# Rotary swap of two attention layers through small transfers, a turn of the identity ahead of long rows of products, and weight halves split earlier on VectorE

## What is computed

```python
def _rope(x, cos, sin):                 # q and k, heads of 64
    x1, x2 = jnp.split(xf, 2, axis=-1)  # halves of 32
    out = jnp.concatenate([x1 * c - x2 * s, x2 * c + x1 * s], axis=-1)
...
for l in range(DEPTH):                  # 2 layers
    h = _swiglu(x, ffn_w1[l, 0], ffn_w3[l, 0], ffn_w2[l, 0])
    x = _layernorm(ALPHA * x + 0.5 * h, ...)
    h = _mixer(x, l, ...)               # z = x @ w_in; q, k = _rope(q), _rope(k); ...
    x = _layernorm(ALPHA * x + h, ...)
    h = _swiglu(x, ffn_w1[l, 1], ffn_w3[l, 1], ffn_w2[l, 1])
    x = _layernorm(ALPHA * x + 0.5 * h, ...)
...                                     # second block: six chunks of silu(c) @ w_mod
```

## Time and profile before

| | us |
|---|---|
| median of three runs | 1831.58 |
| lowest, highest | 1826.11, 1833.10 |
| the profiled execution | 1825.48 |
| its span, on which the trace's times lie | 1823.6 |
| PE busy (98% of the span) | 1789.7 |
| DVE busy (62%) | 1136.4 |
| ACT busy (48%) | 867.9 |
| POOL busy (14%) | 247.0 |

### The profile page before, as it was taken

One profiled execution on the slowest core, in us unless ns is written; L12 is line 12 of the kernel. 1 busy time (PEld: TensorE's weight loads), 2 busy tenths in 40 slices (PEclk: granted clock), 3 DMA queues, 4 the chain that ended last, 5 costly groups with the idle time before them and its releaser, 6 DMA issues.

```text
span 1823.6 us, 31041 instructions
## 1 busy us (share of the span) xinstructions
PE 1789.7 (98%) x12819; PEld 1617.9 (89%) x12819; DVE 1136.4 (62%) x1735; ACT 867.9 (48%) x1412; POOL 247.0 (14%) x264
## 2 busy tenths in 40 slices
PE   9999999999999999999999999999999999999999
PEld 8998699999899879996899997999776877879999
DVE  5754587676766466655675876566655655565553
ACT  5454344664444435443535753545345355445543
POOL 2000232121200020001231212000111443100000
PEclk9999999999999999999999999999999999999999
DMA  8665654545666666754755455775443433346663
GB/s 285 195 219 192 233 186 159 165 139 191 206 208 209 204 208 231 231 185 161 250 169 185 135 168 193 234 242 182 165 152 93 110 98 93 117 159 190 203 194 111
DMA packets 252396, 330.56 MB, mean 181 GB/s; under 512 B 13162, under 2 KB 213072, under 8 KB 252256
## 3 DMA queue, kind: packets, MB, share of 16 engines
q1 hardware_dynamic: 248240, 315.31, 53.2%
q0 software_dynamic: 4016, 13.27, 2.1%
HBM read 327.51 MB, written 1.05 MB: 180 GB/s over the span
## 4 chain that ended last, share of the span: by engine, by line
PE 64%; issue 24%; DVE 6%; POOL 2%; ACT 2%; DMA 1%; POOLq 0%; DVEq 0%; ACTq 0%
PE bank L714 14%; PE bank L717 14%; PE bank L715 14%; PE bank L737 5%; PE bank L739 5%; PE bank L740 5%; DVE X L1930 1%; DVE wlo L1852 1%; ACT whi L1402 1%; PE bank L1250 1%; PE bank L1272 1%; POOL rs L2447 1%; DMA G<-in_lam_dram 1%; PE bank L898 1%; PE bank L936 1%
## 5 line engine op out<-in xcount | busy, mean ns | idle before, releaser
L1852 DVE TENSOR_TENSOR wlo<-raw,whi 128x1024 fp32r<-128x1024 f32 x537 | 663.8, 1241 | 374.6 <-ACT whi L1402 370.5
L1402 ACT ACTIVATE whi<-raw 128x1024 fp32r<-128x1024 f32 x549 | 574.4, 1052 | 393.6 <-PE bank L740 171.7
L714 PE MATMUL bank<-XTh,whi 128*128 128x256 f32 x1984 | 560.7, 283 | 0.0
L717 PE MATMUL bank<-XTh,wlo 128*128 128x256 f32 x1984 | 551.8, 278 | 2.9 <-DVE wlo L1852 2.9
L715 PE MATMUL bank<-XTl,whi 128*128 128x256 f32 x1984 | 551.6, 278 | 0.0
L717 PEld LDWEIGHTS bank<-XTh,wlo 128*128 128x128 f32 x1984 | 372.9, 188 | 3.3 <-DVE wlo L1852 3.3
L715 PEld LDWEIGHTS bank<-XTl,whi 128*128 128x128 f32 x1984 | 374.8, 189 | 1.0
L714 PEld LDWEIGHTS bank<-XTh,whi 128*128 128x128 f32 x1984 | 372.9, 188 | 2.9
L714 PE MATMUL bank<-HCh,whi 128*128 128x256 f32 (+1 forms) x880 | 252.5, 287 | 0.9 <-DVE tmp L2343 0.9
L717 PE MATMUL bank<-HCh,wlo 128*128 128x256 f32 (+1 forms) x880 | 248.1, 282 | 0.0
L715 PE MATMUL bank<-HCl,whi 128*128 128x256 f32 (+1 forms) x880 | 248.1, 282 | 0.0
(11 more groups left out here) (342 smaller groups left out, 2419.6 us busy)
## 6 DMA issues: line engine op xcount, KB each, us to landing
raw<-in_ffn_w_dram SPq DMA_DIRECT2D x131, 1024.0 KB, 5.1
raw<-in_w_in_dram SPq DMA_DIRECT2D x76, 1024.0 KB, 5.0
raw<-in_w_mod_dram SPq DMA_DIRECT2D x24, 1024.0 KB, 5.0
raw<-in_w_branch_dram SPq DMA_DIRECT2D x16, 1024.0 KB, 5.0
raw<-in_w_out_dram SPq DMA_DIRECT2D x12, 1024.0 KB, 4.9
raw<-in_w_ffn_gate_dram SPq DMA_DIRECT2D x11, 1024.0 KB, 5.1
raw<-in_w_ffn_up_dram SPq DMA_DIRECT2D x11, 1024.0 KB, 5.1
raw<-in_w_ffn_down_dram SPq DMA_DIRECT2D x8, 1024.0 KB, 5.1
```

Of the source, the lines that this page charges most:

```text
L714: e.matmul(o, hi[:, k, w0:w0 + nc_], xh, start=first and k == 0, stop=False)
L717: m = e.matmul(o, lo[:, k, w0:w0 + nc_], xh, start=False, stop=last and k == nk - 1)
L1402: e.activation(hi_part(n), raw_part(n), ACTF.Copy).then_inc(WHI.did(n), 1)
L1852: e.tensor_tensor(lo_part(n), raw_part(n), hi_part(n).bitcast(F32), ALU.subtract).then_inc(WLO.did(n), 1)
```

## The change

Three things.

1. **Rotary.** `perm` and its product are gone. The swap of partitions p and p^32 is made by four DMAs of 32 partitions x 256 numbers (32 KB each) from the copy `s` to a buffer `u` of `mtmp`: two are issued by SP (partitions 0 to 63) and two by POOL (64 to 127). The ring has six buffers in place of four. SP issues them between two loads of weights, POOL ahead of its additions. DVE multiplies the copy by cos (`times_cos(n-1)`) and one group later the swapped copy by sin (`times_sin(n-2)`); POOL adds `rotate(n-2)`. ACT's copy of group n now waits for the four DMAs of group n-3.
2. **A turn of the identity.** `settle(b)` transposes the 128 x 128 identity into an unused part of a bank: at the end of each `modulation`, and in each mixer between V and the first q/k group.
3. **Splits ahead of long work on DVE.** `sum_up` does half of a chunk at a time, so a split stands between the halves. `w.more(1)` is called ahead of the second layernorm tile of V on ACT and DVE, and ahead of `g2` on ACT and DVE.

The core of the diff:

```diff
             if self.summed and self.summed[0] < min(self.parts[self.n][0], self.loaded):
-                c = self.summed.pop(0)
-                self.done.add(c)
+                c = self.summed[0]
                 if self.sum_up:
-                    self.sum_up(c)
-                self.load()
+                    self.sum_up(c, self.step)
+                self.step = 1 - self.step
+                if self.step == 0:
+                    self.done.add(self.summed.pop(0))
+                    self.load()
...
+            def turned(l, n):                       # SP
+                ring_free(q, tm[l], ("u", n))
+                q.wait_ge(AMX, ("qk", l, n))
+                for p in (0, 32):
+                    e.dma_start(mtmp[tm[l].slot["u", n]][p:p + 32, :], mtmp[tm[l].slot["s", n]][p ^ 32:(p ^ 32) + 32, :]).then_inc(
+                        ROT[n % 4].did(("turned", l, n), by=16), 16)
...
             for c in range(1, before_bias):
                 load(c)
+                for l in range(2):
+                    if first_qk[l] <= c - 4 < first_qk[l] + 8:
+                        for j in range(2):
+                            turned(l, 2 * (c - 4 - first_qk[l]) + j)
...
+            def settle(b):                          # PE
+                return e.transpose(bank[b][:, 256:384], ident, ident)
...
-                mm.then_inc(MOD.did(("columns", g)), 1)
+                settle(b).then_inc(MOD.did(("columns", g)), 1)
...
+                empty(3)
+                settle(3)
                 for n in range(16):
                     b = n % 4
                     empty(b)
                     gemm_a(bank[b][:, 0:T], xt, ("qk", l, n))
                     emptied[b] = ((AMX, ("qk", l, n)),)
-                    if n:
-                        rotate(n - 1)
...
                 for n in range(16):                 # DVE
                     w.pass_by(1)
                     if n:
-                        rotate(n - 1)
+                        times_cos(n - 1)
+                    if n > 1:
+                        times_sin(n - 2)
+                times_cos(15)
...
+                def turned(n):                      # POOL
+                    ring_free(q, tm[l], ("u", n))
+                    q.wait_ge(AMX, ("qk", l, n))
+                    for p in (64, 96):
+                        e.dma_start(mtmp[tm[l].slot["u", n]][p:p + 32, :], mtmp[tm[l].slot["s", n]][p ^ 32:(p ^ 32) + 32, :]).then_inc(
+                            ROTP[n % 4].did(("turned", l, n), by=16), 16)
                 for n in range(16):
                     w.pass_by(1)
-                    if n:
-                        rotate(n - 1)
+                    turned(n)
+                    if n > 1:
+                        rotate(n - 2)
```

More of the change, by code:

```diff
@@ L379, in program @@
     with ctx:
-        chunks, parts, whole, on_dve, before_bias = plan(I)
+        chunks, parts, whole, on_dve, before_bias, first_qk = plan(I)
         of_chunk = {}
@@ L393, in program @@
         BIAS = [signal(f"s_bias{h}") for h in range(8)]
+        ROT = [signal(f"s_rotary{i}") for i in range(4)]
+        ROTP = [signal(f"s_rotary_pool{i}") for i in range(4)]
         MM, TURN, SMALL, MOD = [signal("s_pe_" + n) for n in ("gemm", "turn", "small", "mod")]
@@ L437, in program @@
         sb(xst, "gap1", [128, 68])
-        cm, cos, sin, perm = csa[:, 0:256], csa[:, 256:512], csa[:, 512:768], csa[:, 768:896]
+        cm, cos, sin = csa[:, 0:256], csa[:, 256:512], csa[:, 512:768]
         def ffn_bufs(st, name, at=STANDS):
@@ L453, in program @@
             G = sb(st, "G", [128, 16, T])
-            mtmp = some(st, "mtmp", 4, [128, T])
+            mtmp = some(st, "mtmp", 6, [128, T])
             sm = sb(st, "sm", [128, 16])
@@ L1475, in mixer @@
                     q.wait_ge(MM, ("V", l, t))
+                    if t:
+                        w.more(1)
                     for c in range(2):
@@ L1860, in sum_up @@
                     q.wait_ge(MOD, ("columns", BEFORE[g]))
-                for k in range(4):
+                for k in (2 * step, 2 * step + 1):
                     for m in range(2) if g < 4 else (k % 2,):
@@ L1956, in mixer, with times_cos, times_sin @@
                     e.scalar_tensor_tensor(V[:, t, :], V[:, t, :], rs[:, t, 1:2], gb[:, 1, :], ALU.mult, ALU.add).then_inc(DMX.did(("v", l, t)), 1)
-                def rotate(n):
-                    b, dst, j, scale = 4 + n % 2, (Q, K)[n // 8], n % 8, (0.125, 1.0)[n // 8]
-                    u = mtmp[tm[l].slot["u", n]]
-                    q.wait_ge(SMALL, ("perm", l, n))
-                    ring_free(q, tm[l], ("u", n))
-                    e.scalar_tensor_tensor(u[:, :], bank[b][:, 0:T], scale, sin, ALU.mult, ALU.mult).then_inc(DMX.did(("sin", l, n)), 1)
+                def times_cos(n):
+                    dst, j, scale = (Q, K)[n // 8], n % 8, (0.125, 1.0)[n // 8]
+                    q.wait_ge(AMX, ("qk", l, n))
                     e.scalar_tensor_tensor(dst[:, j, :], mtmp[tm[l].slot["s", n]][:, :], scale, cos, ALU.mult, ALU.mult).then_inc(
                         DMX.did(("cos", l, n)), 1)
+                def times_sin(n):
+                    u, scale = mtmp[tm[l].slot["u", n]], (0.125, 1.0)[n // 8]
+                    q.wait_ge(ROT[n % 4], ("turned", l, n))
+                    q.wait_ge(ROTP[n % 4], ("turned", l, n))
+                    e.scalar_tensor_tensor(u[:, :], u[:, :], scale, sin, ALU.mult, ALU.mult).then_inc(DMX.did(("sin", l, n)), 1)
                 for n in range(16):
```

50 lines of the change are left out of this document (20 added, 30 removed).

## The result

The changed kernel took 1822.06 us in the median of nine runs (1817.79 to 1826.52), beside 1831.58 for the kernel before (nine runs, 1825.05 to 1838.11). The ratio is 0.9949, with a 95% interval from 0.9930 to 0.9967: 9 us faster, not the 21 us of the prediction, and inside its range of 1802 to 1824 only by 2 us. In a later comparison the same kernel gave 0.9973 (0.9957 to 0.9990), 5 us. The mean of the two is some 7 us.

The account below looks back on a forecast made before the run. PE, busy 98% of the span, was taken as the bound. Rotary 14.0, modulation turns 5.4, sum_up 2.0 and g2 −0.7 gave 20.7 us off 1825.5, so 1804.8; plus 6.1 for the median, 1810.9 us, range 1802 to 1824.

Parts of the forecast that it names:

- the loop: Rotary step behind group 6: POOL's two DMA issues and addition take 2.7 us against PE's 2.72 per group, and it holds.
- rival 2: Rotary step: the loop through POOL and the DMAs is too long, 3 to 4 us lost per layer, 1817 to 1819; chance 0.12.
- the pace of q/k: Rotary stage: slow q/k and u groups become fast behind the turn, 2.1 us gained per layer.
- The products with `perm`: Rotary stage: removing 16 products per layer saves 0.44 us each, 7.0 us per layer.
- The wait at group 4: Rotary stage: PE newly waits 1.6 us per layer for the low half that DVE makes behind V's layernorm.
- At group 6: Rotary stage: PE newly waits 1.4 us per layer, as DVE's product with sin awaits POOL's DMAs queued behind gb.
- rivals 2 and 3: Rival 3, rotary step: POOL at over twice its issue time; 1.3 us per issue eats all 20.7; chance 0.04.
- The turn ahead of q/k: Between V and q/k: one turn makes the slow groups fast, 2.1 us gained per layer, the turn itself costing 0.1.
- Rival 1: Modulations and q/k: the turn doesn't switch the pace, 1821 us, or 1815 to 1817 if one site switches; chance 0.22.
- The turns behind the modulations: Rows behind the five modulations: 1344 products go from slow to fast, 6.0 us less the turns' cost, 5.4 gained.
- `sum_up` and `g2`: Attention: halves of sum_up gain 2.0 us (0 to 2.9); the split ahead of g2 loses 0.7.
- `more(1)` in V's layernorm: V's layernorm: calling it ahead of the second tile moves nothing, 0 us.

Follow-up runs that it names:

- banks: The changed kernel with sgu in four banks in place of two, gb still loaded ahead of the rotary step: 0.9916 (0.9892 to 0.9941) of the kernel before.
- gb_banks: The changed kernel with POOL's two gb loads moved behind the rotary step and sgu in four banks: 0.9879 (0.9856 to 0.9902) of the kernel before.
- no_swap: The changed kernel without the rotary step's small transfers, DVE multiplying the unswapped copy by sin: 0.9845 (0.9821 to 0.9870) of the kernel before.
- act_queue: gb_banks with SP's two small transfers per group issued by ACT right behind its copy: 0.9905 (0.9881 to 0.9929) of the kernel before.

## Why the prediction was wrong

**The failed step: `sgu` taken as a cover.** The stage was to go from 56.4 us by 7.0 + 1.0, with 3.0 given back. What DVE's lateness costs behind group 6 has no term in the sum; it stands at nothing, on the ground that the loop "holds". In rival 2 I subtracted `sgu`'s 4.0 us as time in which DVE could catch up. But PE needs DVE inside `sgu`: it fills two banks and then waits until DVE has emptied the first. I followed DVE's lateness only to the next low half, where four parts of lead hide it, and not to the next place where PE needs DVE with less lead. The wait there is 3.5 and 3.0 us. It also lowers the clock; the stretches behind it, in the changed kernel, with PEclk the third number from the end:

```profile
279.20:284.70 5.50, 1.99 (x18) 1.80 (x17) 5.03 (x10) 1.33 (x2) 4.88 (x7) 0.98 0.88 288
284.70:288.00 3.30, 3.28 (x16) 3.28 (x17) 1.38 (x4) 0.00 (x0) 0.40 (x1) 0.52 0.08 21
```

Half of 3.3 at the lower level of 1.2 GHz is 1.6: together 5 us in the first layer alone. The two stages were expected at about 50 us each, and took 57.7 and 57.1. With the wait for DVE out of the way, and `gb`'s, they take 48.8 and 50.2.

**The clock behind group 6.** The sum has the two waits there but not what the clock does behind them. In the second layer, behind the wait of 2.8 us, it fell too:

```profile
909.10:912.50 3.40, 3.40 (x18) 3.40 (x17) 3.40 (x5) 1.47 (x3) 3.08 (x6) 0.50 0.37 91
```

That is another 1.7 us. Together: 6.5 for the waits in `sgu`, 5 for three stretches at the lower clock (this one and one behind each wait in `sgu`), and 4.2 for the pace of q/k (below) are 16 of the forecast 20.7; 9 and 5 were measured. With four banks alone the two waits in `sgu` and the clock behind them fall out, and the forecast less the 4.2 is 16.5; the kernel `banks` gave 15, from 11 to 20. The products with `perm` were priced a little high: the q/k part took 52.6 us before and 45.4 in `gb_banks`, with one wait of 1.0 in each, and 0.8 of the difference is pace. That leaves 6.4 per layer, forecast 7.0.

**The wait at group 4** was 1.0 us in each layer, forecast 1.6: PE ran at the slow pace and came later. **At group 6** it was 2.1 and 2.8, forecast 1.4. The mechanism is the one forecast: POOL's transfers behind `gb`, DVE's product with sin ahead of the low half. What was mis-sized is the landing of `gb`, taken from the earlier trace rows as 5.2; in `no_swap`, without the small transfers, it is 5.9, and here 6.3:

```profile
gb<-in_ln_b_dram POOLq DMA_DIRECT2D x1, 512.0 KB, 6.3
```

**The loop.** "On the edge, but it holds" is right for POOL and beside the point. POOL's issues took 0.5 each, so rivals 2 and 3 through POOL's issue time fall. Rival 2's other condition, longer landings, came in part: POOL's pair landed in 4.4 (median, first layer) in place of 3.8. (Its sum also has a slip: 6.6 less 4.0 is 2.6 per layer, not 3 to 4.) It is DVE that had no slack: 2.35 us per group against 2.72 to 2.83, and SP's pair, for which I saw 0.4 to spare, lost it as soon as DVE was late once, since SP's next load waits for DVE's low halves and the pair lands behind that load.

**The turn ahead of q/k** was to be worth 2.1 us per layer. It is worth nothing. With one turn behind the 512-wide products of V the first group was slow in 13 of 14 layers (seven profiled executions with it), and without a turn in all ten. I had counted 19 turns of 19 as evidence, and none of them stood behind wide products; the six cases that did had no turn. Nor did the 19 hold where they came from. Behind the three turns of attention, 16 of 16 rows were fast in the trace of before, but 12 of 16 in the first trace of the changed kernel and 10 to 15 in the kernels built on it. Behind the one turn ahead of the second row of 384 (L870 before, L888 after; an expectation above calls it a single product) the row was slow in 5 of the 14 profiled executions. The perfect count of one execution was luck. Rival 1 allowed for "one of the two sites", with 1815 to 1817, and that is what happened to this term.

**The turns behind the modulations** are right, though the evidence that they were taken from was not: 50 of 50 such rows fast in the ten profiled executions with the turn, 18 of 20 slow in the four without. 6.0 us less 0.6, and the kernel with this alone is at least 5.3 us faster. The Trainium skill's single gap of 109 ns ("TensorE: Matmul & The Clock Gate", section "Back-to-back issue gap") has no place for this gain; both paces are there in every trace of this case, at 113 to 114 and 117.8 ns.

**`sum_up` and `g2`** are right in size: the sum of both was 1.3 us, measured 1.3 with an interval of 2 us to each side. `g2` alone cost 1.3 in its stretch, forecast 0.7, and the wait (5.5) and the clock (0.50) behind it came as said. `more(1)` in V's layernorm did nothing.

**The base.** I set the sum against one profiled execution and added 6.1 us for the median. Part of that 6.1 may be the drawn pace; no trace of a median run of the kernel before shows it. A row of 384 products and the one of 1188 are fast in the trace of before and slow in the first trace of the changed kernel: 1572 products at 4.45 ns are 7.0 us. That is why its span is only 1.8 us shorter while the medians are 9 apart. A term of 2 us is not to be read from one pair of spans here.

Terms, as forecast and as measured: rotary −14.0, and +2.4 (interval 0 to 5) for it alone; modulations −5.4, and −8.4 (−11.7 to −5.3); `sum_up` and `g2` −1.3, and −1.3. The sum of what was measured apart is −7.3, the change as a whole −9.3 and −4.9.

## What to carry to other kernels

When a step makes an engine late, follow its lateness past the first consumer to every place where the bottleneck needs it with less lead, such as a pair of banks that it must empty; a stage that "covers" the lateness is no cover if it needs the late engine itself. Small transfers that others wait for belong on an engine and a queue without large loads ahead of them, and the loads that nobody needs yet belong behind. A pattern that correlates with a fast state in one trace (a turn, here) may be chance, even at 19 of 19, and says nothing of other kinds of work; a second execution of the same kernel is a cheap test.

## What the runs showed of the hardware

- **Two paces, drawn.** Dense 128x256 products start every 113 to 114 ns or every 117.8, for a row of up to 1188, and the same row of the same program comes out at either in two executions (5.3 us apart). The summed cost of slow rows was between 6 and 22 us in the profiled executions, as much as the spread of the kernel's runs (1825 to 1838). What draws it stays open; only the 16 short products of a modulation with a single turn behind them gave the fast one always (50 of 50).
- **A small transfer issued behind a 1 MB load on SP's queue** lands in 4.0 us (median), and from ACT's queue in 2.9. Single ones spread widely on either: 1.8 to 6.9 us in `gb_banks`, 1.8 to 6.0 in `act_queue`.
- **DVE beside POOL.** DVE's product with cos takes 0.42 us alone (at 242.93) and 0.96 while POOL adds, which it does from 252.96 on:

```profile
252.96 1.04 POOL L2493 TENSOR_TENSOR Q<-Q,mtmp 128x256 f32<-128x256 f32 x1
```

  The Trainium skill has this ("SBUF — State Buffer", section "Who interferes with whom": a DVE instruction with two inputs in SBUF contends with a GpSimd instruction that reads SBUF, and the later one waits), and the trace agrees in kind: 0.54 us of waiting inside the operation. The rule of that page which I had weighed, that DVE can starve POOL's issue of transfers, is stated there for DVE's 2-port modes, and this section says that `tensor_tensor`, which makes the low halves, has no such mode; the prediction missed that. The trace agrees: POOL's issues took 0.50 to 0.54 us each in the first trace of the changed kernel, with DVE's two-input operations beside them.
- **The clock behind a wait.** The granted clock was 0.50 to 0.52, the level of 1.2 GHz, in the 3.2 us and more behind the waits of 2.8, 3.5 and 5.5 us, and stayed at 1.00 behind the one of 2.1:

```profile
251.10:254.50 3.40, 3.39 (x28) 3.39 (x29) 3.40 (x5) 2.43 (x4) 2.80 (x5) 1.00 0.24 69
```
